# RWKV-7 chunk stage on one Trainium2 core: a dense fp32 matmul on constants at the head of every merge and product job, and two of 512 columns behind the last one

## The reference, cut to what matters

```python
def step(state, inp):
    r_t, w_t, k_t, v_t, kk_t, a_t = inp
    sa = einsum('bhvk,bhk->bhv', state, -kk_t)
    state = state * w_t[..., None, :] + sa[..., None] * (kk_t * a_t)[..., None, :] \
            + v_t[..., None] * k_t[..., None, :]
    return state, einsum('bhvk,bhk->bhv', state, r_t)
```

## Time and profile before

| | us |
|---|---|
| median of 3 runs | 3276.66 (3276.38 to 3277.37) |
| profiled execution, whole | 3270.4 |
| its span | 3268.6 |
| PE busy, of the span | 2870.4 (88%) |
| DVE busy | 1469.9 (45%) |
| ACT busy | 782.3 (24%) |
| mean granted clock of PE | 0.857 |

### The profile page before, as it was taken

The page is one execution under the profiler, slowest core; times in us unless marked ns, Lnnn a source line. Parts: engine busy times, 40 slices in busy tenths (PEclk is TensorE's granted clock), DMA queues, the critical chain, the costliest instruction groups (busy, mean ns, idle before and its releaser), DMA issues. The chain is left out here.

```text
span 3268.6 us, 47367 instructions
## 1 busy us (share of the span) xinstructions
PE 2870.4 (88%) x18974; PEld 2642.3 (81%) x18974; DVE 1469.9 (45%) x2799; ACT 782.3 (24%) x1527; POOL 105.2 (3%) x165
## 2 busy tenths in 40 slices
PE   4599999999996999579689688786889999999995
PEld 2289999999995998266476575666789999999995
DVE  1453333333437661382563745733364433333335
ACT  1231111111104111333243433322141111111112
POOL 0000000000000000001102001010000000000000
PEclk7799999999997999765665655657889999999997
DMA  8511111111101232111010110104111111111101
GB/s 350 208 52 39 39 39 39 51 39 50 40 7 40 82 96 106 76 24 31 18 23 24 25 39 3 34 5 162 39 49 42 45 39 39 39 39 51 39 19 58
DMA packets 190799, 182.69 MB, mean 56 GB/s; under 512 B 43956, under 2 KB 163551, under 8 KB 190687
## 3 DMA queue, kind: packets, MB, share of 16 engines
q1 hardware_dynamic: 190416, 180.97, 17.1%
q10 hardware_dynamic: 270, 0.09, 0.0%
HBM read 153.05 MB, written 27.98 MB: 55 GB/s over the span
## 5 line engine op out<-in xcount | busy, mean ns | idle before, releaser
L126 PE MATMUL ff_ps<-h_hi,ff_wlo 128*128 128x384 f32 x2112 | 710.7, 336 | 5.6 <-ACT ff_s L602 5.6
L127 PE MATMUL ff_ps<-h_lo,ff_whi 128*128 128x384 f32 x2112 | 709.9, 336 | 0.0
L128 PE MATMUL ff_ps<-h_hi,ff_whi 128*128 128x384 f32 x2112 | 709.6, 336 | 0.0
L650 DVE TENSOR_TENSOR ff_s<-ff_ps,ff_s 128x384 f32<-128x384 f32 x132 | 73.5, 557 | 750.0 <-PE ff_ps L128 748.7
L126 PEld LDWEIGHTS ff_ps<-h_hi,ff_wlo 128*128 128x128 f32 x2112 | 400.2, 189 | 6.2 <-ACT ff_s L602 6.2
L127 PEld LDWEIGHTS ff_ps<-h_lo,ff_whi 128*128 128x128 f32 x2112 | 399.8, 189 | 0.0
L128 PEld LDWEIGHTS ff_ps<-h_hi,ff_whi 128*128 128x128 f32 x2112 | 399.7, 189 | 0.0
L128 PE MATMUL ff_ps<-ff_uhi,ff_whi 128*128 128x384 f32 x1056 | 352.7, 334 | 0.0
L127 PE MATMUL ff_ps<-ff_ulo,ff_whi 128*128 128x384 f32 x1056 | 352.7, 334 | 0.0
L126 PE MATMUL ff_ps<-ff_uhi,ff_wlo 128*128 128x384 f32 x1056 | 352.7, 334 | 0.0
L602 ACT ACTIVATE ff_s<-ff_ps 128x384 f32<-128x384 f32 x132 | 65.1, 493 | 738.4 <-PE ff_ps L128 738.4
(11 more groups left out here) (269 smaller groups left out, 3759.4 us busy)
## 6 DMA issues: line engine op xcount, KB each, us to landing
md_w<-w_mod SPq DMA_DIRECT2D x9, 4096.0 KB, 24.6
ff_raw<-ffn_w_gate SPq DMA_DIRECT2D x44, 512.0 KB, 4.6
ff_raw<-ffn_w_up SPq DMA_DIRECT2D x44, 512.0 KB, 3.9
ff_raw<-ffn_w_down SPq DMA_DIRECT2D x44, 512.0 KB, 3.7
pj_raw<-w_in SPq DMA_DIRECT2D x19, 512.0 KB, 4.0
z_dram<-pj_zo SPq DMA_DIRECT2D x15, 576.0 KB, 2.9
rw_rkv<-z_dram SPq DMA_DIRECT2D x12, 576.0 KB, 5.6
x_dram<-x SPq DMA_DIRECT2D x1, 4608.0 KB, 21.7
```

What stands on the lines that cost most here:

```text
L126: pe.matmul(out, w_lo, x_hi, start=start, stop=False)
L127: pe.matmul(out, w_hi, x_lo, start=False, stop=False)
L128: return pe.matmul(out, w_hi, x_hi, start=False, stop=stop)
L650: dve.tensor_tensor(hid[:, t % 2, :], ps[:, 2 + t % 2, 0:CW], silu[:, t % 2, :], ALU.mult)\
```

## The change

Four things in the PE part of `rw_chunks`, and nothing on another engine:

- `keep_clock` takes the number of columns, and the number of matmuls last.
- Every `f`, `w`, `u` and `y` job issues one matmul of 128 columns on constants (128 rows, 128 stationary columns) into its own bank, ahead of its own products. In `w`, `u` and `y` jobs it also stands ahead of the waits for other jobs' copies; in the first `f` job of a direction it stands behind the wait for DVE.
- The four matmuls of 512 columns ahead of each direction stay.
- Behind the last job PE waits for the copy of the job eight places from the end, and issues two matmuls of 512 columns.

That is 30 matmuls of 128 columns and two of 512 per stage, 120 and 8 in all.

```diff
--- before.py
+++ after.py
@@ -128,10 +128,10 @@
     return pe.matmul(out, w_hi, x_hi, start=False, stop=stop)
 
 
-def keep_clock(pe, sb, out, n):
+def keep_clock(pe, sb, out, columns, n=1):
 
     for _ in range(n):
-        pe.matmul(out, sb["cst"][:, C_ID:C_ID + P], sb["cst"][:, 0:512], start=True, stop=True)
+        pe.matmul(out[:, 0:columns], sb["cst"][:, C_ID:C_ID + P], sb["cst"][:, 0:columns], start=True, stop=True)
 
 
 def parts(c):
@@ -1600,19 +1600,22 @@
                                              start=True, stop=True)
                     elif k == "f":
                         if q == 0:
-                            keep_clock(pe, sb, out, 4)
+                            keep_clock(pe, sb, out, 512, 4)
                             dve_t.wait(pe, f"nat{d}_1")
+                        keep_clock(pe, sb, out, P)
                         for j in range(NF):
                             u = q * NF + j
                             last = pe.matmul(out[second(d), j * B:(j + 1) * B], gu[first(d), d, u, second(d)],
                                              nat[d][first(d), u, :], start=True, stop=True)
                     elif k == "w":
+                        keep_clock(pe, sb, out, P)
                         copied(pe, "f", d, q)
                         for j in range(NF):
                             u = q * NF + j
                             last = pe.matmul(out[first(d), j * B:(j + 1) * B], fs[d][second(d), u * B:(u + 1) * B],
                                              wu[second(d), d, u, second(d)], start=True, stop=True)
                     elif k == "u":
+                        keep_clock(pe, sb, out, P)
                         copied(pe, "z", d, q)
                         copied(pe, "w", d, q * NU // NF)
                         for j in range(NU):
@@ -1629,6 +1633,8 @@
                                 last = pe.matmul(out[HS * h:HS * h + HS, j * HS:(j + 1) * HS],
                                                  at[:, d, c, HS * h:HS * h + HS], rw.wt[:, d, h, c, :], start=True, stop=True)
                     pe_t.did(name(k, d, q), last)
+                copied(pe, *jobs[-8])
+                keep_clock(pe, sb, ps[:, len(jobs) % 8, :], 512, 2)
 
             def copy_out(eng, tr, k, d, q, copy, neg):
```

## The result

| us | before | after |
|---|---|---|
| median of 4 runs each | 3276.52 (3275.04 to 3277.37) | 3398.80 (3393.22 to 3399.24) |
| span of the profiled execution | 3268.6 | 3391.4 |
| PE busy | 2870.4 | 2986.7 |
| DVE busy | 1469.9 | 1469.6 |
| mean granted clock of PE | 0.857 | 0.845 |

The ratio of the runs is 1.037, with a 95% interval of 1.0352 to 1.0388: the kernel became 3.7% slower, by 122 us. The forecast was 3365 with a range of 3304 to 3392. The direction was right, and the time lies above the range.

The account below looks back on a forecast made before the run. PE was taken to bound the chunk stages, at half clock in d=0; 9.75 + 10.1 + 3.1 = 22.9 us a stage, less 1 for the scan, about 22 x 4 = +88 us, gave 3365 us, range 3304 to 3392.

Parts of the forecast that it names:

- What bounds the stage: Chunk stages: PE and DVE reach d=1 within 0.33 us, so extra PE work in d=0 is late in full.
- The clock: Chunk stages: d=0 stays at 0.50; d=1 has full clock for some 6 us, then 0.50 from the last merge jobs.
- Rivals 1 and 2: Chunk stages: d=1 at full clock to its end (3308 to 3329, 0.17); both directions so (3281 or 3290, 0.09).
- rival 1: d=1 of each chunk stage stays at full clock to its end: 3308 to 3329 us, chance 0.17.
- The price of one dense matmul: Each added 128-column matmul at a job's head: 0.65 us at half clock, 0.40 us at full clock.
- the seam: Extra time where small products hand over to a dense matmul and back, seen in the trace with a semaphore wait.
- The close: Two 512-column matmuls at each stage's end, less 0.55 us of cover: +3.1 us at half clock, +1.4 at full.
- The discount of 1 us for a hot start of the scan: Scan behind each chunk stage may begin with some us at full clock: 1 us a stage taken off.
- The upper end: Top of the range: dense matmul at 0.85/0.50 us gives 28.8 us a stage, +115 in all, 3392 us.
- lower end: Bottom of the stated range, 3304 us; the range leaves out both directions hot, the faster case and times above.

Follow-up runs that it names:

- d=0 alone: Dense 128-column matmuls at the heads of the d=0 jobs only, d=1 and closing as in the kernel before: 3331.36 us, +56.
- d=0 hot: Kernel before with ten 512-column dense matmuls ahead of d=0, twelve ahead of d=1, two inside each direction: 3288.85 us.
- the close alone: Kernel before plus only the two 512-column matmuls behind the last job, none at job heads: 3288.39 us against 3275.66, +12.7.

## Why the prediction was wrong in size, point by point

- **What bounds the stage: right.** PE and DVE arrive together at d=1, so that d=0 counts in full (+56 us from d=0 alone), and a faster d=0 gains nothing (25.2 us against 25.4 with d=0 hot).
- **The clock: right.** d=0 at 0.50, full clock for the first 4.5 to 5.8 us of d=1, 0.50 for the rest. Rivals 1 and 2 did not come. One reading against rival 1 was loose: the prediction has the clock of the kernel before fall "while `w` and `u` ran", and in all four stages it fell in `u`, 1.2 to 1.4 us behind its start. Its price took 6.66 us for `u`, where the earlier trace rows have 6.74 from start to start, which changes nothing.
- **The price of one dense matmul: this step failed.** It was bounded by 0.46 and 0.85 us at half clock, and 0.65 was taken "between the ends", because the seam had been seen with a semaphore wait in it. It measured 0.86 to 0.91, above even the upper bound. The wait has no part in it (0.85 in the middle of a job); the seam is the change of shape, 0.43 us of it. The rule of the Trainium skill quoted beside it ("TensorE: Matmul & The Clock Gate", what overlaps and what doesn't) pointed to the upper end, where the price came out. The trace agrees with it for the dense matmul, whose first load came late, and not for small products: the load of the own shape ran beside a product on the same 32 rows and cost no seam. At full clock 0.52 was measured where 0.40 was taken. On 15 + 15 jobs in four stages that is d=0 +13.3 in place of +9.75 and d=1 +12.8 (without its first head, which stands in the row above it in the table) in place of +10.1, together some 25 us of the 34 by which the forecast of +88 us fell short.
- **The close: right**, 3.2 us in the first stage for 3.1 (2.5 to 3.2 over the four), and +12.7 us by itself.
- **The discount of 1 us for a hot start of the scan: wrong.** With the close alone the scans began at full clock in all four stages, with the whole change in three, and none of the stretches measured behind them was shorter by 1 us. That is 4 us.
- **The upper end.** It was made of the upper price and gave 28.8 us a stage, +115; the stages show +116. The range ended there, with nothing for what lies outside of them. The span grew by 6.6 us more: 0.35 ahead of the first stage's d=0, 2.6 in the three stretches from one chunk stage's end to the next one, 3.6 behind the last. No instruction was added there. With other kernels of the study the three stretches differ from those before by -2.2 to +5.4 us in sum, without a pattern, and runs of the kernel before spread over 12.9 us, so 6.6 us between two profiled executions may be no more than that. The cause stays open. Both ends of the range were summed without the discount of 1 us that the forecast has, and its lower end, 3304, lies 4 us under rival 1's 3308 with no reason given.

## What to carry to other kernels

A bound that comes from the one place in the trace where the same hand-over happens is not an end of a range but the estimate; take the middle only with a reason that was measured. A dense matmul of 128 columns dropped between small ones cost its columns plus a seam of the same size. What paid in this kernel was warm-up work in one or two long pieces, ahead of the place where the clock had been lost, and in a stretch whose end PE sets. Raising the clock and holding it are separate questions: read in the trace which work does the one and which the other.

## What the runs showed of the hardware that was not expected

- The same work can hold a full clock that it doesn't raise: 64x64 fp32 products ran 6.6 us at 1.00 behind a dense matmul of 512 columns at full clock, and 512-column matmuls at the head of every job stayed 51.7 us at 0.50 in d=0 and 30.2 us at 1.00 in d=1 of the same stage.
- A matmul of 128x128 stationary and 32 moving columns among 32x32 products costs 0.70 us at half clock, hardly less than with 128 moving columns (0.86); one of 128 columns in the products' own shape costs 0.43.
- Whether one dense matmul of 512 columns carries the clock over `w` differs from stage to stage of one execution (3 of 4), at the same place in the program.
